# Cumulated gates behind the bisection, the last score tile one tile later, and a new order in the first gate and up group

## The reference, cut to what matters

```
h = modulate(rms_norm(x, norm_attn_g), sh1, sc1)
proj = h @ w_in                                  # 7 column groups of 512 (the index group is narrower)
# sparse attention: which 256 keys a query may see
score = sum over 4 heads of relu(iq @ ik) * iw,  causal;   idx = top_k(score, 256)
# forgetting attention: a bias from cumulated gates
log_f = log_sigmoid(f_logit + b_forget);  cum = cumsum(log_f, axis=seq)
logits = q @ k / 8 + cum[query] - cum[key]
...
x = x + g1 * (concat(norm(o_d), norm(o_f)) @ w_out)
h = modulate(rms_norm(x, norm_ffn_g), sh2, sc2)
x = x + g2 * ((silu(h @ w_gate) * (h @ w_up)) @ w_down)
```

## Time and profile before

| | us |
|---|---|
| median of three runs | 1376.49 (1376.42 to 1378.89) |
| profiled execution, its own time | 1376.04 |
| its span | 1374.3 |
| PE busy | 1307.8 (95% of the span) |
| DVE, POOL, ACT busy | 980.2, 773.7, 710.1 |

### The profile page before, as it was taken

One profiled execution on the slowest core, in us unless ns is written; L12 is line 12 of the kernel. 1 busy time (PEld: TensorE's weight loads), 2 busy tenths in 40 slices (PEclk: granted clock), 3 DMA queues, 4 the chain that ended last, 5 costly groups with the idle time before them and its releaser, 6 DMA issues.

```text
span 1374.3 us, 19543 instructions
## 1 busy us (share of the span) xinstructions
PE 1307.8 (95%) x6595; PEld 1070.2 (78%) x6595; DVE 980.2 (71%) x1585; ACT 710.1 (52%) x1427; POOL 773.7 (56%) x518
## 2 busy tenths in 40 slices
PE   1999999999999999999999999999999999999996
PEld 0988778888877777778887788888888888788884
DVE  4563769999777878766569666555555666479998
ACT  6623446666387788873344344333344343554545
POOL 0251426645006200530028899888888993898985
PEclk8899999999999999999999999999999999999999
DMA  9131324443569998724110433223333235998873
GB/s 385 54 100 54 123 79 151 153 140 114 136 159 236 318 275 255 230 63 169 47 46 16 146 115 111 73 94 107 109 115 115 95 113 164 394 351 302 287 238 155
DMA packets 138124, 219.42 MB, mean 160 GB/s; under 512 B 11725, under 2 KB 66181, under 8 KB 137002
## 3 DMA queue, kind: packets, MB, share of 16 engines
q1 hardware_dynamic: 138026, 218.18, 48.7%
HBM read 166.43 MB, written 51.71 MB: 159 GB/s over the span
## 4 chain that ended last, share of the span: by engine, by line
PE 76%; DVE 9%; issue 4%; ACT 4%; DMA 3%; POOL 2%; SPq 1%; DVEq 0%; ACTq 0%; POOLq 0%
PE PS L2193 21%; PE PS L2194 20%; PE PS L2195 20%; PE PS L2408 4%; PE PS L2362 4%; DVE AS L2059 2%; PE PS L2379 2%; DMA ada<-in_ada_w_dram 2%; DVE BS L2064 1%; POOL WSf L1039 1%; PE PS L2384 1%; ACT LP L1285 1%; PE PS L2381 1%; DMA adar<-in_ada_w_dram 1%; DMA rawa<-gu_scratch 1%
## 5 line engine op out<-in xcount | busy, mean ns | idle before, releaser
L1364 ACT CAST WS<-WSf 128x512 fp32r<-128x512 f32 x110 | 68.5, 623 | 204.4 <-POOL WSf L1039 203.6
L1051 POOL TENSOR_TENSOR WS<-WSf,WS 128x512 fp32r<-128x512 f32 x109 | 163.5, 1508 | 4.4 <-ACT WS L1364 4.4
L1039 POOL TENSOR_TENSOR WSf<-rawg 128x512 f32<-128x512 f32 x55 | 79.1, 1438 | 118.9 <-PE PS L2195 113.9
L2193 PE MATMUL PS<-yh,WS 128*128 128x512 f32 (+2 forms) x360 | 140.7, 391 | 1.5 <-DVE yl L1973 1.5
L2194 PE MATMUL PS<-yl,WS 128*128 128x512 f32 (+2 forms) x360 | 140.3, 390 | 0.0
L2195 PE MATMUL PS<-yh,WS 128*128 128x512 f32 (+2 forms) x360 | 140.0, 389 | 0.0
L2193 PE MATMUL PS<-BS,AS 128*128 128x512 f32 x308 | 120.4, 391 | 4.1 <-DVE BS L2064 2.2
L2195 PE MATMUL PS<-BS,AS 128*128 128x512 f32 x308 | 119.9, 389 | 0.0
L2194 PE MATMUL PS<-BS,AS 128*128 128x512 f32 x308 | 119.9, 389 | 0.0
L1285 ACT ACTIVATE LP<-LP,nmin 128x128 f32<-128x128 f32 (+7 forms) x128 | 100.3, 783 | 33.5 <-DVE nmin L1832 32.2
L2059 DVE TENSOR_TENSOR AS<-rawa,AS 128x512 fp32r<-128x512 f32 x77 | 99.1, 1304 | 24.9 <-ACT AS L1423 24.7
(11 more groups left out here) (339 smaller groups left out, 3774.9 us busy)
## 6 DMA issues: line engine op xcount, KB each, us to landing
rawb<-in_w_down_dram SPq DMA_DIRECT2D x132, 256.0 KB, 4.8
rawa<-gu_scratch SPq DMA_DIRECT2D x77, 256.0 KB, 4.6
gu_scratch<-GS SPq DMA_DIRECT2D x55, 256.0 KB, 4.6
raw<-in_w_in_dram SPq DMA_DIRECT2D x24, 512.0 KB, 4.2
rawg<-in_w_gate_dram SPq DMA_DIRECT2D x22, 512.0 KB, 4.3
rawu<-in_w_up_dram SPq DMA_DIRECT2D x22, 512.0 KB, 4.3
ada<-in_ada_w_dram SPq DMA_DIRECT2D x8, 1024.0 KB, 15.0
qk_scratch<-stageh SPq DMA_DIRECT2D x32, 256.0 KB, 2.0
```

The lines of the kernel that those rows point to most:

```text
L1039: pool.tensor_tensor(WSf[m % N_SLOT][:], left(i, mat, a), left(i, mat, b), ALU.add if sign > 0 else ALU.subtract).then_inc(ws_sum, 1)
L1051: pool.tensor_tensor(lo, WSf[m % N_SLOT][:] if b else left(i, mat, a), hi.bitcast(F32), ALU.subtract).then_inc(ws_ready, 1)
L1364: act.copy(WS[m % N_SLOT][:, 0], src).then_inc(ws_hi, 1)
L2193: pe.matmul(dst, left[0], right[0], start=first, stop=False)
```

## The change

The last score tile (token tile 7) moves from (2, 4) to (2, 5), and the counts start at (2, 5), one tile earlier, instead of (2, 6). The cumulated gates leave (2, 6) and are formed in two parts behind (6, 3) and (6, 4); on DVE their sums stand behind `settle`, the low part behind the choice of two token tiles. The store and the loads of `cum_scratch` move in SP's order behind the store of (6, 4). In the first pair forms "6" and "7" of gate come ahead of those of up, so that gate's "7" is product 11 and up's "6" is product 12. ACT rounds slots 4 and 5 earlier.

```diff
-SCORE_TILES = (0, 1, 2, 3, 5, 6)
-COUNT_TILE = 8
+SCORE_TILES = (0, 1, 2, 3, 5, 7)
+COUNT_TILE = 7
+FORGET_AT = ((NC - 1, 3), (NC - 1, 4))
 ...
-    between[divmod(at, TT)] = [("forget",)]
 ...
             order += between.get((ch, t), [])
+            if (ch, t) in FORGET_AT:
+                order.append(("forget", FORGET_AT.index((ch, t))))
 ...
-            for first, last in ((0, 2), (2, 4), (4, 5), (5, 6), (6, N_FORM)):
+            for first, last in ((0, 2), (2, 4), (4, 5), (5, N_FORM)):
 ... SP
                     if ch == 6 and t == 1:
                         sp.wait_ge(strip_ok, 4)
-                        sp.wait_ge(cum_out, 16)
-                        load_cum(0)
-                        load_cum(1)
 ...
+                    if ch == 6 and t == 4:
+                        sp.wait_ge(cumT_ok, 2)
+                        sp.dma_start(cum_dram..., cumT[:].bitcast(F32)).then_inc(cum_out, 16)
+                        sp.wait_ge(cum_out, 16)
+                        load_cum(0)
+                        load_cum(1)
 ...
-                if ch == 4:
-                    sp.wait_ge(cumT_ok, 2)
-                    sp.dma_start(cum_dram..., cumT[:].bitcast(F32)).then_inc(cum_out, 16)
 ... ACT
-            def forget():
-                act.wait_ge(cum_pe, 1)
-                act.copy(cumq[:], PS[:, 4, 0:NH * TT]).then_inc(cum_ev, 1)
+            def forget(part):
+                if part == 0:
+                    act.wait_ge(cum_pe, 1)
+                    act.copy(cumq[:], PS[:, 4, 0:NH * TT]).then_inc(cum_ev, 1)
+                    return
                 act.wait_ge(cumT_pe, 1)
                 act.copy(cumT[:, 0, :], PS[0:NH * TT, 5, 0:P]).then_inc(cumT_ok, 1)
-                act.wait_ge(cumT_ok, 2)
 ...
                 if s == TT - 1:
-                    for m in range(4):
+                    for m in range(5):
                         slot_high(m)
                 if s < TT:
                     root2(s)
+                if s == TT - 1:
+                    slot_high(5)
                 if s >= 1:
                     scale2(s - 1)
-            for m in range(4, N_SLOT):
-                slot_high(m)
+            slot_high(6)
 ... DVE
+            for i in range(BISECT):
+                bisect(i)
+            settle()
             dve.wait_ge(fg_a, 2)
             (log gates and running sums, L1796 to L1800, as before)
+            advance(2 * CHOICE_OPS)
             dve.wait_ge(cumT_pe, 1)
             (low part of cumT, L1803, as before)
-            for i in range(BISECT):
-                bisect(i)
-            settle()
-            advance(CHOICE_EARLY)
+            advance(CHOICE_EARLY - 2 * CHOICE_OPS)
 ... PE
-            def cumulative():
-                pe.wait_ge(sc_done, IH * (TT - FIRST_TOPK))
+            def cumulative(part):
+                if part == 1:
+                    pe.wait_ge(cum_ev, 1)
+                    pe.transpose(PS[0:NH * TT, 5, 0:P], cumq[:], ident[:]).then_inc(cumT_pe, 1)
+                    return
+                pe.wait_ge(sign_cnt, len(SIGN_TILES) * BISECT)
                 pe.wait_ge(fg_v, 4 + TT)
                 (two products, L2308 and L2309, as before)
-                pe.wait_ge(cum_ev, 1)
-                pe.transpose(PS[0:NH * TT, 5, 0:P], cumq[:], ident[:]).then_inc(cumT_pe, 1)
```

More of the change, by code:

```diff
@@ L732, in _ @@
                         load_qk(0)
+                    if ch == 6 and t == 4:
+                        sp.wait_ge(cumT_ok, 2)
+                        sp.dma_start(cum_dram.rearrange("a h (t p) -> (h t) a p", p=P), cumT[:].bitcast(F32)).then_inc(cum_out, 16)
+                        sp.wait_ge(cum_out, 16)
+                        load_cum(0)
+                        load_cum(1)
                     if ch == 6 and t == 5:
@@ L736, in _ @@
                         load_qk(1)
-                if ch == 4:
-                    sp.wait_ge(cumT_ok, 2)
-                    sp.dma_start(cum_dram.rearrange("a h (t p) -> (h t) a p", p=P), cumT[:].bitcast(F32)).then_inc(cum_out, 16)
             def load_mod(n):
@@ L1233, in _ @@
                 elif step[0] == "forget":
-                    forget()
+                    forget(step[1])
                 elif step[0] == "angles":
@@ L2326, in _ @@
                 elif step[0] == "forget":
-                    cumulative()
+                    cumulative(step[1])
                 elif step[0] == "angles":
```

## The result

The kernel after took 1367.97 us (median of 5 runs, 1362.98 to 1369.97) against 1376.42 us for the kernel before (5 runs, 1374.98 to 1378.89): ratio 0.9926, 95% interval 0.9907 to 0.9946. The prediction was 1365.2 us, a ratio of 0.9918. Its profiled execution was its fastest run: 1362.98 us, span 1361.2 us.

The account below looks back on a forecast made before the run. PE was taken as the bound. Projection 5.7 (4.66 + 1.0) and feed-forward 5.6 (6.43 - 0.8) sum to 11.3 us off the profiled 1376.04: 1364.7, with the median 0.45 above at 1365.2; range 1363.5 to 1370.5.

Parts of the forecast that it names:

- Score tile 7 (4.66): Projection: PE's wait for DVE's first head of tile 7 (2.46 us) and slow matmuls behind it go, gain 4.66 us.
- gates (1.0): Projection at (2, 6): PE's wait of 0.9 us for ACT's copy is hidden, gain 1.0 us, bounds 0.6 and 1.5.
- 2.20 us for the slow matmuls at the scores: Projection: 12 matmuls behind the score wait take 4.91 us instead of 2.71; this 2.20 us was expected to go.
- My first rival: The clock falls all the same, behind the new wait of 0.96 us; costs up to 2.95 us, time 1368.2, chance 0.17.
- Settling (331.5, bounds 329.5 to 335.6): End of the bisection: settling starts at 331.5 us; 329.5 if PE's tiles rule, 335.6 if the chain's own pace does.
- nearer to the tiles: Settling's start taken as 331.5 us, since the chain catches up wherever a tile holds one count.
- my own sign (settling after 335): Stated sign of being wrong: settling of the bisection starts after 335 us.
- PE's visit: PE comes for the gates' sums behind tile (6, 3) at 340.7 us; sums there at 337.6, spare 3.1.
- Store and loads: SP's rows of the gates: store lands 3.7 us after issue, at 352.2; loads land at 355.4, 2.1 us to spare.
- The second rival (rows of the gates last): Settling at 335.6, loads land at 358.6 to 363.5 against attention at 357.5; time 1368.7 us, chance 0.12.
- Order of gate and up (6.43): First pair: stall ahead of product 13 goes, product 11 waits 0.96 us for `x_low(2)`; row's end 6.43 us earlier.
- ACT's early slots (-0.8): Feed-forward: a POOL sum meeting DVE's scaling of tile 7 delays everything up to product 11, a loss of 0.8 us.

Follow-up runs that it names:

- ff_half: The kernel before with only the feed-forward part (order of the first gate and up group, ACT's slots 4 and 5 earlier): 1369.94 us, ratio 0.9949.
- before_again: The kernel before, unchanged, run for a second trace: 1378.46 us, one run.
- gates_alone: The kernel before with only the cumulated gates moved, counts and last score tile as they were: 1376.68 us, ratio 0.9990.
- low_memset: The kernel after with POOL's low part of the projection tiles replaced by a memset of the same tile: 1367.71 us, ratio 0.9942.
- no_early_slots: The kernel after with ACT's slots 4 to 6 rounded in their old place, behind `scale2`: 1368.58 us, ratio 0.9942.
- no_reorder: The kernel after with the first pair's old product order: 1370.73 us, ratio 0.9961.
- low_first: The kernel after with the old product order, and POOL's low part of slot 13 ahead of the sum of slot 14: 1369.61 us, ratio 0.9938.
- score_alone: The kernel before with only the last score tile moved, from (2, 4) to (2, 5): 1378.68 us, ratio 1.0013.

## Why the prediction was right

**Score tile 7 (4.66) and gates (1.0).** The sum of 5.7 is what the two traces show: 231.5 to 225.8. The split was wrong. I read two waits as two prices, and they are two ends of one chain on DVE. Moving the score tile alone gains nothing; only with the gates out of the way does its wait go. The prediction gave the score tile its gain by asking what PE needs next from DVE's heads, and didn't ask when the sums behind `signed(7)` come against PE's new place.

**The clock.** I took 2.20 us for the slow matmuls at the scores, as if it belonged to the wait. The fall followed the wait of 2.31 us in 2 of 4 traces (before, ff_half; not before_again, gates_alone), the 1.5 us at the last split in 3 of 6, and the 3.1 to 3.4 us at product 13 in 5 of 6. With the fall the projection takes 231.3 or 231.5, without 229.9: a fall costs 1.5 there. Gate and up take 434.1 or 434.0 with both falls, 432.7 or 432.8 with the one at product 13 and 431.0 with none. My first rival, a fall behind the new wait, came in one trace of five with the full wait (low_memset: 427.9 against 426.2). Over the traces of each kind the projection gains 230.65 - 225.9 = 4.8 (gates_alone counted with 1.0 added) and gate and up 432.9 - 426.6 = 6.3. That is 11.1, close to the forecast's 11.3, and less than the 5.7 + 7.9 of the two traces.

**Settling (331.5, bounds 329.5 to 335.6).** It started at 335.88 (335.2 without the later start of this trace), at the late bound, so the step "nearer to the tiles" failed. The chain's own pace ruled, for a reason that I had the number for and didn't look at: the meeting of POOL and DVE in most steps (in the kernel before too the bound's instruction, L1729, took 0.95 us in the median, and 0.17 without a meeting). Without it settling is at 328.84. By my own sign (settling after 335) I should be wrong, and PE's 0.25 us to spare shows how near it was. What saved it is luck in part. I had PE's visit right (341.25 against 340.7, less than the later start of this trace). But with my 2.7 us for the sums PE would have waited 0.7 us from this start of settling. They took 1.7, since the seven additions took 1.44 us and not the 2.44 of the earlier trace rows.

**Store and loads.** The choices ended at 350.26 instead of 346.9, so the low part was 2 us late. The store gave that back: 2.12 us from its issue to SP's next instruction (350.58 to 352.70), not the 3.7 of the earlier trace rows. The loads were issued by 353.83 and the logits at 358.18 did not wait. The Trainium skill (DMA: Bandwidth & Descriptors, "Anatomy of one DMA"), whose fixed cost of about 2.0 us was measured on DMAs that GpSimd issues and not SP, was nearer than the row of before, which I had preferred. The time goes with the store's place: 3.6 to 4.0 us in the four traces that have it in the old one, 0.5 us behind two other stores (286.71 in the kernel before), and 2.1 or 2.2 in the ten that have it in the new one, 2.6 us behind the last (after). No run moves the store alone, so that the stores ahead of it are the cause isn't shown. The second rival (rows of the gates last) didn't come, since it took 3.7 and up to 6.9 for what took 2.1 and less than 4.4.

**Order of gate and up (6.43).** 6.3 by no_early_slots, with the wait on `x_low(2)` at 0.9. The cause that I named, POOL's low part behind a sum that waits for a late load, is shown by no_reorder (stall back) and low_first (stall gone, the late load still felt). Of its two halves the late load weighs more: the queue order alone gives back 1.5 of 4.9.

**ACT's early slots (-0.8).** The sign was wrong: 434.1 - 6.3 = 427.8 became 426.2, a gain of 1.6. The meeting that I foresaw happened, and DVE's scaling of tile 7 rose from 0.75 to 1.59 us. But it fell into DVE's wait for ACT, and POOL was idle when the last split began. I had named that case ("or nothing if POOL's idle stretch behind frees a DVE instruction") and had not taken it. The step that failed is "PE would only come sooner to product 11, and that waits for `x_low(2)`": `x_low(2)` hangs on the same split, so it came sooner too: product 11 starts 37.1 us behind product 0 instead of 38.8. The prediction held product 11's date fixed while moving the work that sets it.

**Sum.** Two errors nearly cancel, and that is luck. The early slots were 2.4 better than charged (-0.8, it was +1.6). The falls counted in full were some 2.5 too much: the two traces show 5.7 + 7.9 = 13.6, the means over all traces 11.1. Against the medians, 8.4 and 9.8 us, the forecast of 11.3 was 1.5 to 2.9 too large; the stages sum to 11.1. The rest stays open. The down stage takes 225.7 to 226.4 in the four traces with neither half whole (before, before_again, score_alone, gates_alone) and 226.8 in the mean of the nine that hold the projection's change, but 224.2 in ff_half. What differs there is PE's two waits for `BS`, on POOL and on DVE: 2.1 us together in ff_half, 3.2 to 4.7 in the other traces of up to 226.4, 4.6 to 5.7 in those of 226.6 and more. What sets their length I can't tell from chance.

## What to carry to other kernels

Two waits of one engine on one other engine's queue are one chain until an experiment parts them: date what the second needs with the first one gone. When a step is moved ahead, move also the dates of everything that hangs on it before saying that the gain is lost in the next wait. Charge a slow clock behind a wait by how often it follows in several traces, not by the one trace at hand.

## What the runs showed of the hardware

A wait of one length is followed by the lower clock in some executions and not in others: 2.31 us in 2 of 4, 1.5 us in 3 of 6. In attention the same holds for a wait of PE on ACT that comes in kernels with and without each half of the change: the wait and the stretch from 440 to 448 us, in ff_half and then in gates_alone.

```profile
442.23 1.09 PE L2363 MATMUL PS<-ident,LP 128*128 128x128 f32 x8 [1.73 <-ACT PTa L1275]
...
440.00:448.00 8.00, 6.27 (x34) 5.07 (x36) 5.49 (x12) 6.97 (x18) 7.86 (x5) 0.79 1.03 283
```

```profile
440.52 1.09 PE L2368 MATMUL PS<-ident,LP 128*128 128x128 f32 x8 [1.73 <-ACT PTa L1278]
...
440.00:448.00 8.00, 7.48 (x53) 6.20 (x54) 5.25 (x16) 7.18 (x19) 7.85 (x5) 1.00 1.03 310
```

Of the seven traces in which this wait is 1.7 us the clock falls behind it in six; in the five in which it is 0.7 to 1.0 us (both traces of the kernel after among them) it doesn't. Attention takes 350.7 to 352.7 us without a fall and 354.0 to 355.5 with one, the longer wait included. How much of the spread between executions of one kernel comes from such falls isn't shown: the two traces of the kernel after have none at these places and differ by 3.0 us, 1.8 of it in the down stage.

A DVE instruction of 0.17 us took 1.16 where it met one of POOL. The Trainium skill (SBUF — State Buffer, "SBUF: two separate sides") says that the one that starts first holds the shared ports for its whole length and the other is blocked; the trace agrees, as L1733 starts 0.14 us behind POOL's 1.29 us and ends with it. I had not expected that a handshake between engines can lock such a meeting into nearly each turn of a loop.
